# A mixture-of-experts layer on one core: six slots for the high parts of the weights, low parts written over their raw slots, five high parts ahead

## The reference

```
def _moe(h, w_router, b_router, w_gate, w_up, w_down):
    ...
    scores = jax.nn.sigmoid((hf @ w_router).astype(jnp.float32))
    ...
    for e in range(N_EXPERTS):
        he = jax.nn.silu(hf @ w_gate[e]) * (hf @ w_up[e])
        y = y + combine[:, e:e + 1] * (he @ w_down[e])
    return y.reshape(B, T, D).astype(h.dtype)
```

## Time and profile before

| | |
|---|---|
| median of 3 runs | 769.23 us (768.83 to 771.93) |
| span of the profiled execution | 769.4 us |
| PE busy, share of the span | 738.5 us, 96% |
| DVE | 587.7 us, 76% |
| ACT | 429.6 us, 56% |
| POOL | 95.5 us, 12% |
| moved by DMA | 172.72 MB, mean 224 GB/s |

### The profile page before, as it was taken

The page is one execution under the profiler, slowest core; times in us unless marked ns, Lnnn a source line. Parts: engine busy times, 40 slices in busy tenths (PEclk is TensorE's granted clock), DMA queues, the critical chain, the costliest instruction groups (busy, mean ns, idle before and its releaser), DMA issues. The chain is left out here.

```text
span 769.4 us, 10991 instructions
## 1 busy us (share of the span) xinstructions
PE 738.5 (96%) x4051; PEld 601.2 (78%) x4051; DVE 587.7 (76%) x817; ACT 429.6 (56%) x514; POOL 95.5 (12%) x131
## 2 busy tenths in 40 slices
PE   6899999999999999999999989999999999999994
PEld 5777999987877776878888757888888888888872
DVE  6967999797763545434666789888998999899988
ACT  5643344255445454652230246787788778887855
POOL 4010000000110000000000246311121111212002
PEclk9999999999999999999999999999999999999998
DMA  8547313420273111151349949999999999999163
GB/s 282 169 132 257 109 56 110 165 70 1 94 294 110 55 55 56 57 217 55 110 122 388 333 143 363 406 392 402 393 401 391 403 394 393 389 404 385 44 243 137
DMA packets 98547, 172.72 MB, mean 224 GB/s; under 512 B 15264, under 2 KB 35056, under 8 KB 98188
## 3 DMA queue, kind: packets, MB, share of 16 engines
q1 hardware_dynamic: 91200, 153.10, 55.2%
q0 software_dynamic: 4896, 12.95, 4.3%
q10 hardware_dynamic: 2412, 6.15, 2.1%
HBM read 161.83 MB, written 21.10 MB: 238 GB/s over the span
## 5 line engine op out<-in xcount | busy, mean ns | idle before, releaser
L2044 DVE TENSOR_TENSOR m_lo<-m_raw,m_hi 128x2048 fp32r<-128x2048 f32 x95 | 214.9, 2289 | 26.0 <-ACT m_hi L1008 22.9
L1008 ACT ACTIVATE m_hi<-m_raw 128x2048 fp32r<-128x2048 f32 x95 | 179.1, 1917 | 22.9 <-PE low L1156 22.4
L1154 PE MATMUL low<-m_hi,xe_hi 128*128 128x512 f32 x256 | 102.7, 401 | 0.7 <-DVE xe_lo L2180 0.5
L1156 PE MATMUL low<-m_hi,xe_lo 128*128 128x512 f32 x256 | 100.0, 391 | 0.0
L1155 PE MATMUL low<-m_lo,xe_hi 128*128 128x512 f32 x256 | 99.8, 390 | 0.0
L1154 PE MATMUL low<-hT_hi,w_hi 128*128 128x512 f32 (+1 forms) x240 | 94.5, 394 | 3.1 <-ACT smallT L767 1.2
L1155 PE MATMUL low<-hT_lo,w_hi 128*128 128x512 f32 (+1 forms) x240 | 92.0, 383 | 0.0
L1156 PE MATMUL low<-hT_hi,w_lo 128*128 128x512 f32 (+1 forms) x240 | 91.6, 382 | 0.0
L1731 DVE TENSOR_TENSOR w_lo<-raw,w_hi 128x2048 fp32r<-128x2048 f32 x27 | 61.8, 2290 | 37.2 <-ACT w_hi L737 37.0
L737 ACT ACTIVATE w_hi<-raw 128x2048 fp32r<-128x2048 f32 x28 | 53.5, 1909 | 16.5 <-PE wide L1156 8.3
L1154 PEld LDWEIGHTS low<-m_hi,xe_hi 128*128 128x128 f32 x256 | 48.1, 188 | 14.1 <-DVE m_lo L2044 3.7
(11 more groups left out here) (424 smaller groups left out, 1419.7 us busy)
## 6 DMA issues: line engine op xcount, KB each, us to landing
m_raw<-in_w_gate SPq DMA_DIRECT2D x32, 1024.0 KB, 8.0
m_raw<-in_w_up SPq DMA_DIRECT2D x32, 1024.0 KB, 7.9
m_raw<-in_w_down SPq DMA_DIRECT2D x31, 1024.0 KB, 8.3
raw<-in_w_in SPq DMA_DIRECT2D x19, 1024.0 KB, 5.7
raw<-in_w_out SPq DMA_DIRECT2D x4, 1024.0 KB, 5.1
y<-y_dram SPq DMA_DIRECT2D x8, 512.0 KB, 6.5
table_dram<-table_row ACTq DMA_DIRECT2D x1, 2624.0 KB
strips<-table_dram SPq DMA_DIRECT2D x8, 264.0 KB, 4.1
```

Of the source, the lines that this page charges most:

```text
L1008: nc.scalar.activation(m_hi[n % MS][:, :], (m_spare if is_last(n, j) else m_raw[slot])[:, :], ACT.Copy).then_inc(q["m_hi_ready"], 1)
L1154: nc.tensor.matmul(outp, lh, rh, start=first, stop=False)
L1156: return nc.tensor.matmul(outp, ll, rh, start=False, stop=last)
L2044: v.tensor_tensor(m_lo[n % MS][:, :], (m_spare if is_last(n, j) else m_raw[n % MR])[:, :], m_hi[n % MS][:, :].bitcast(F32), ALU.subtract). ...
```

## The change

`MS` goes from 3 to 6. The three new high slots lie where the three low slots were. A low part is now written over its own raw unit, in place; the last one over `m_spare`, under the name `spare_lo`. Since the slot then holds the low part until PE has used it, everything that waited for "low part made" in order to use a raw slot anew waits for "PE has used it": SP's refills, its loads of `g2`, `b2` and of the results, and DVE's `last_sel`. At the start, ACT makes five high parts ahead of the first rows in place of three, and the sixth right behind the first `xe_hi`.

```diff
-MR, MS = 12, 3
+MR, MS = 12, 6
...
-        m_hi = [at(f"m_hi{i}", [P, UNIT], F32R, x) for i, x in enumerate((A0 + 8, A0 + 16, A0 + 24))]
-        m_lo = [at(f"m_lo{i}", [P, UNIT], F32R, x) for i, x in enumerate((0, 8, 16))]
+        m_hi = [at(f"m_hi{i}", [P, UNIT], F32R, x) for i, x in enumerate((A0 + 8, A0 + 16, A0 + 24, 0, 8, 16))]
+        m_lo = [at(f"m_lo{i}", [P, UNIT], F32R, A0 + (32 + 8 * i if i < MR - 1 else 0)) for i in range(MR)]
+        spare_lo = at("spare_lo", [P, UNIT], F32R, A0 + 136.5)
...
                 for slot in range(MR):
                     e, part = order[MR + slot]
-                    sp.wait_ge(q["m_lo_ready"], j * MR + (slot + 1 - MR))
+                    sp.wait_ge(q["m_used"], j * MR + (slot + 1 - MR))
                     m_load(j * 2 + (e - 2), part, slot)
             for slot in range(MR - 1):
                 u = MU * NE - MR + slot
-                sp.wait_ge(q["m_lo_ready"], u + 1 - MR)
+                sp.wait_ge(q["m_used"], u + 1 - MR)
                 m_load(*order[u], slot)
 
-            sp.wait_ge(q["m_lo_ready"], MU * NE - MR + 7)
+            sp.wait_ge(q["m_used"], MU * NE - MR + 7)
...
             sp.wait_ge(q["all_scattered"], 1)
-            sp.wait_ge(q["m_lo_ready"], MU * NE - MR + 4)
+            sp.wait_ge(q["m_used"], MU * NE - MR + 4)
             results_load()
...
-            m_split_hi(0)
-            m_split_hi(1)
-            m_split_hi(MS - 1)
+            for n in range(MS - 1):
+                m_split_hi(n)
...
-            m_split_hi(3)
+            m_split_hi(MS - 1)
             silu_gate(0, 2)
-            m_split_hi(4)
             act.wait_ge(q["xe_done"], 2)
...
-            def m_unit(u, s, outp, part, x_hi, x_lo):
+            def m_unit(u, n, outp, part, x_hi, x_lo, low=None):
 
                 pe.wait_ge(q["m_lo_ready"], u)
-                wh = m_hi[s][:, :].rearrange("p (c n) -> p c n", c=4)
-                wl = m_lo[s][:, :].rearrange("p (c n) -> p c n", c=4)
+                wh = m_hi[n % MS][:, :].rearrange("p (c n) -> p c n", c=4)
+                wl = (low or m_lo[n % MR])[:, :].rearrange("p (c n) -> p c n", c=4)
...
                 dve.wait_ge(q["m_hi_ready"], j * MR + (n + 1))
-                v.tensor_tensor(m_lo[n % MS][:, :], (m_spare if is_last(n, j) else m_raw[n % MR])[:, :], m_hi[n % MS][:, :].bitcast(F32), ALU.subtract).then_inc(q["m_lo_ready"], 1)
+                v.tensor_tensor((spare_lo if is_last(n, j) else m_lo[n % MR])[:, :], (m_spare if is_last(n, j) else m_raw[n % MR])[:, :],
+                                m_hi[n % MS][:, :].bitcast(F32), ALU.subtract).then_inc(q["m_lo_ready"], 1)
...
             for i in range(3):
                 m_split_lo(MU + i, j)
-            dve.wait_ge(q["m_lo_ready"], MU * NE - 4)
+            dve.wait_ge(q["m_used"], MU * NE - 4)
             v.tensor_tensor(last_sel[:, :, :], count_up[:, :].rearrange("p (o x) -> p o x", o=1).to_broadcast([P, TT, P]),
```

More of the change, by code:

```diff
@@ L536, in _ @@
             with sp.If(over > P):
-                sp.wait_ge(q["m_lo_ready"], 6 * NE)
+                sp.wait_ge(q["m_used"], 6 * NE)
                 sp.wait_ge(q["part_ready"], 4)
@@ L1077, in _ @@
             nc.scalar.activation(xe_hi[:, 0:4, :], bank[6][:, :].rearrange("p (c x) -> p c x", c=4), ACT.Copy).then_inc(q["xe_half_hi"], 1)
-            m_split_hi(5)
             act.wait_ge(q["m_used"], 4)
@@ L1621, in _ @@
                 pe.wait_ge(q["xe_lo_ready" if u else "xe_half_lo"], 1)
-                m_unit(u + 1, u % MS, bank[u // 2][:, :], u % 2, xe_hi, xe_lo)
+                m_unit(u + 1, u, bank[u // 2][:, :], u % 2, xe_hi, xe_lo)
             hidden(0)
@@ L1628, in expert_pe @@
                 pe.wait_ge(q["xe_lo_ready"], j * 2 + (2 + s))
[L1629 to L1632, removed]
+                m_unit(j * MR + (n - 1), n - 2, bank[0][:, :], 0, xe_hi, xe_lo)
+                m_unit(j * MR + n, n - 1, bank[0][:, :], 1, xe_hi, xe_lo)
+                m_unit(j * MR + (n + 1), n, bank[1][:, :], 0, xe_hi, xe_lo)
+                m_unit(j * MR + (n + 2), n + 1, bank[1][:, :], 1, xe_hi, xe_lo)
                 tokens(s, j * 16 + 32)
@@ L1636, in expert_pe @@
                 pe.wait_ge(q["y_out"], j * 2 + (1 + s))
-                m_unit(j * MR + (n + 3), 2, bank[4][:, :], None, hd_hi, hd_lo)
-                m_unit(j * MR + (n + 4), 0, bank[5][:, :], None, hd_hi, hd_lo)
+                m_unit(j * MR + (n + 3), n + 2, bank[4][:, :], None, hd_hi, hd_lo)
+                m_unit(j * MR + (n + 4), n + 3, bank[5][:, :], None, hd_hi, hd_lo)
                 hidden(e)
@@ L1646, in _ @@
             pe.wait_ge(q["xe_lo_ready"], NE)
-            m_unit(u, 1, bank[0][:, :], 0, xe_hi, xe_lo)
-            m_unit(u + 1, 2, bank[0][:, :], 1, xe_hi, xe_lo)
+            m_unit(u, u - 1, bank[0][:, :], 0, xe_hi, xe_lo)
+            m_unit(u + 1, u, bank[0][:, :], 1, xe_hi, xe_lo)
             pe.wait_ge(q["hd_lo_ready"], NE - 1)
             pe.wait_ge(q["y_out"], NE - 1)
[L1651 to L1654, removed]
+            m_unit(u + 2, u + 1, bank[4][:, :], None, hd_hi, hd_lo)
+            m_unit(u + 3, u + 2, bank[5][:, :], None, hd_hi, hd_lo)
+            m_unit(u + 4, u + 3, bank[1][:, :], 0, xe_hi, xe_lo)
+            m_unit(u + 5, u + 4, bank[1][:, :], 1, xe_hi, xe_lo)
             pe.wait_ge(q["hid_ready"], NE)
@@ L1667, in _ @@
             pe.wait_ge(q["m_lo_ready"], u + 6)
-            wh, wl = (t[1][:, :].rearrange("p (c n) -> p c n", c=4) for t in (m_hi, m_lo))
+            wh, wl = (t[(u + 5) % len(t)][:, :].rearrange("p (c n) -> p c n", c=4) for t in (m_hi, m_lo))
             for k in range(4):
@@ L1672, in _ @@
             mm.then_inc(q["m_used"], 1)
-            m_unit(u + 7, 2, bank[5][:, :], None, hd_hi, hd_lo)
+            m_unit(u + 7, u + 6, bank[5][:, :], None, hd_hi, hd_lo, spare_lo)
             pe.wait_ge(q["lists_ready"], 6)
```

## The result

| | kernel before | changed kernel |
|---|---|---|
| median of the runs | 770.02 us (768.83 to 773.43, 22 runs) | 772.06 us (769.64 to 773.54, 22 runs) |
| ratio | | 1.0018, 95% interval [1.0010, 1.0026] |
| span of the profiled execution | 769.4 us | 770.2 us |

The change makes the kernel slower by a little: the ratio is 1.4 us, the means of these runs are 1.3 us apart and their medians 2.0. Three sets of runs together (46 of the changed kernel) have a mean of 771.64 us; 138 runs of the kernel before have 770.34 and a median of 770.15. The distance of the means is 1.3 us (95% interval 1.0 to 1.6). The forecast was 769.8 us, range 768.2 to 771.4: the median lies 0.7 above the range.

A forecast was written before the change was run, and what follows sets the result against it. PE was taken to bound the expert loop and DVE the end. Terms 0 + 0 + 0 + 0.6 = +0.6 us on 769.4 gave 770.0 us for a profile, 769.8 us for the runs, range 768.2 to 771.4.

The forecast's parts named there:

- The base of the sum: Whole kernel: profiled span 769.4 us, median of three runs 769.23, so the runs' forecast was put at 769.8 us.
- the term for the end: End of the program: `last_sel`'s later wait delays PE's unit 93 and so the last store, +0.6 us, bounds 0 to 1.4.
- Forecast +0.65 at `hid`: Last expert: low part 93 late, PE starts unit 93 0.56 us later, its first matmul holds 0.09 more.
- no longer held by the result loads: End: the last `part` begins at 745.1 us, following PE instead of waiting for the result loads.
- Six slots: Expert loop: ACT's 22.4 us of waits on PE go, PE notices nothing; 0 us, bounded by PE's 3.7 us.
- Rival 1: Expert loop: the 0.09 us gap per expert closes, gaining 1.2 to 3.7 us; 766.1 to 768.6 us, chance 0.07.
- the rule of the Trainium skill: Expert loop: a repeating gap on the saturated engine can mean too few buffers; twice the slots would gain 1.2 to 3.7 us.
- which no buffer frees: Expert loop: the late high part stands behind `ye` and `hd_hi` in ACT's order, so more slots gain 0 us.
- Five high parts ahead: Start: two more pieces of 1.9 us fit in ACT's idle 7.84 us, leaving 4 us of cover; 0 us.
- low part in place: DVE: the low part written over its raw slot keeps its instruction shape, 2.29 us each; 0 us.
- later refills: SP's weight loads: issued 2.8 to some 5 us later, with a lead of 30.6 us, 17 us over; 0 us.
- rival 2: Weight loads: refills on PE's count land after their high part is due; 789 us, or +5 for one, chance 0.05.

The follow-up runs named there:

- experiment 2: Changed kernel with `last_sel` moved behind low part 93: 770.74 us, ratio 1.0005 (before 770.30); its repeat 769.75 us, ratio 1.0000 (before 770.27).
- 1: Kernel before with one edit, `last_sel` waits until PE has used unit 91: 770.79 us, ratio 1.0002; again 770.69 us, ratio 1.0011.
- 4: Kernel before plus one unused DVE subtract of two SBUF operands behind low part 93: 770.70 us, ratio 1.0003 (before 770.30).
- 3: Changed kernel with `last_sel` behind low part 93, three high slots and ACT's old order at the start: 770.19 us, ratio 0.9997.
- the old start of 9 to 12: Changed kernel with `last_sel` behind low part 93 and three high parts ahead at the start, six slots kept: 770.35 us, ratio 1.0000.

## Why the prediction failed

**The base of the sum was wrong.** This is the step that failed: "the median of the runs is 769.23, so nothing to speak of lies around it", from which the 769.8 was made. 769.23 was a median of three runs. Over 138 runs the kernel's median is 770.15, 0.9 above it. And something does lie around the span: in each of the 269 runs whose span is known (as 770.0 with a span of 768.3), the time is the span plus 1.7 to 1.9 us. So a span of 769.4 meant a run of 771.2 us, one of the longer ones; it was read as the middle. That the span exceeded the median of the runs, which it is a part of, should have told me that this profile and that median didn't belong together. With 770.15 the same working gives 770.8 us for the changed kernel, and a range of the same width, 769.2 to 772.4, would have held the result.

The base is not the whole miss of 2.3 us (772.06 - 769.8), though. It is 0.9 of it, and the term for the end another 0.15. Of the other 1.2, 0.4 is that this comparison's median lies above the 771.65 of all 46 runs, and some 0.7 is distance between the two kernels for which the sum had nothing and the traces show nothing: forecast +0.6, traces +0.75, medians of all runs +1.5, means +1.3. That part stays open.

**`last_sel`: right mechanism, a term slightly too small.** Forecast +0.65 at `hid`; the trace has 0.56: PE's unit 93 began 0.43 late (3.15 - 2.72) and not 0.56, and its first matmul held PE 0.33 us, 0.10 more, as reckoned. Forecast 1.4 later relative to PE: 734.73 against PE's 734.53, so 0.20 behind unit 92, where it was 1.22 ahead (733.04 against 734.26): 1.42. PE's new wait for low part 93 came. What the sum left out is POOL: "no longer held by the result loads" was wrong, since they came 0.8 us later themselves. The end costs 0.75 us over eleven profiles (0.65 in the first pair), 0.15 more than the sum's 0.6.

**Six slots: right, 0.** The waits of ACT went from 22.4 us to none, and PE's stayed at 13. Rival 1, and the rule of the Trainium skill (Perfetto Trace Analysis, Optimization Strategy) on gaps that repeat, did not happen by more buffers alone: PE's busy time in the ten-expert window went from 178.42 to 178.50 us, and the timed runs of experiment 2 and its repeat lie 0.1 us from before. But the rule was half right. It was the order on ACT that held the late part, as the prediction had it; that order could be changed only with more slots. With three, high part n+6 needs PE to be done with unit n+3, for which `ye` itself waits, so it can't stand ahead of `ye`. I stopped at "which no buffer frees" and didn't ask what the buffers would allow.

**Five high parts ahead, low part in place, later refills: right, 0.** The first `xe_hi` came at 457.26 (457.29 before); ACT's idle time ahead of it fell from 7.84 to 4.26 us, so 3.6 of the cover was used. The 0 of these parts holds in the traces; whether the open distance of the timed runs belongs to one of them isn't shown. ACT at the start:

```profile
442.38 9.10 ACT L1009 ACTIVATE m_hi<-m_raw 128x2048 fp32r<-128x2048 f32 x5
451.50 1.28 ACT L1045 ACT_TABLE_LOAD   x1
457.26 0.60 ACT L1070 ACTIVATE xe_hi<-wide 128x512 fp32r<-128x512 f32 x1 [4.26 <-PE wide L1579]
```

SP's weight loads wait for PE now, as forecast, and no high part waits for them: ACT has no wait for a load of `m_raw` in the stage (rival 2 did not happen). SP's queue in the stage:

```profile
SPq L496 <- PE low L1154: 155.1, 57, 24.8
SPq L496 <- PE wide L1154: 69.1, 26, 3.3
```

**What stays open.** The traces give the changed kernel +0.75 us, the runs +1.3 (1.0 to 1.6). The slow pace of the loop (243.88 in place of 243.54, 0.35 us) showed in all five profiles of the changed kernel and of it with `last_sel` moved, in three of five of the kernel before and its two variants (1 and 4), and in neither of the two with the old start (3 and the old start of 9 to 12). If that is no accident, early high parts bring it about more often, and it adds up to 0.1 to 0.2 us on average; twelve profiles don't prove it, and `last_sel` moved with the new start is not slower for it in the runs (+0.1). Nor does the clock's dip at 50 us, ahead of all that the edits touch, look like the reason. The timed runs have no trace, but each has its mean granted clock: 0.9923 over the 46 runs of the changed kernel, 0.9921 over the 116 of the kernel before for which it is known. About 0.4 us of the distance of the means has no place (1.3 - 0.75 - 0.15; with the interval, 0.1 to 0.7).

## What to carry to other kernels

A wait that moves from one's own counter to that of another engine costs what stands behind it in the in-order queue, not the instruction itself: put such an instruction behind the one that somebody waits for (one line, 0.75 us). More buffers take away waits, but not order; when a gap survives them, look which instruction stands ahead of the late one, and whether the new buffers now let it pass (1.6 us here, where the slots alone gave nothing). And before a sum is made in tenths, see that the base is known to tenths: hold the profile's span against the runs, and distrust a median of three.

## What the runs showed of the hardware

- **A DVE instruction with two SBUF operands holds up POOL's scatter.** The DMA_INDIRECT takes 0.97 us when DVE idles, 1.87 when it starts 1.3 us into a low part, 1.70 beside a subtraction of 128x1024, 1.16 beside `last_sel`, and ends 0.85 us behind the DVE instruction each time. A DVE instruction with one operand in PSUM doesn't: in the kernel before, a gather takes 1.00 us in the middle of an `xe_lo`. A 128x1 copy on POOL shows both: 1.87 us when a low part had just begun (it ends with it), 0.20 beside an `hd_lo`, which reads PSUM:

```profile
504.75 1.00 POOL L640 DMA_INDIRECT xg<-h_dram,now_source  x1 [0.79 <-POOL now_source L637]
504.44 1.22 DVE L2120 TENSOR_TENSOR xe_lo<-wide,xe_hi 128x1024 fp32r<-128x1024 f32 x1
...
708.91 1.87 POOL L696 COPY now_result<-result_row 128x1 int32<-128x1 int32 x1
708.45 6.81 DVE L2044 TENSOR_TENSOR m_lo<-m_raw,m_hi 128x2048 fp32r<-128x2048 f32 x3 [0.85 <-ACT m_hi L1008]
...
725.80 0.20 POOL L696 COPY now_result<-result_row 128x1 int32<-128x1 int32 x1
725.58 0.69 DVE L2129 TENSOR_TENSOR hd_lo<-low,hd_hi 128x512 fp32r<-128x512 f32 x1
```

  The Trainium skill (SBUF — State Buffer, Terms) says that DVE and GpSimd share a pair of ports that is locked for a whole instruction, and that the loser blocks. By that rule the traces agree.
- **The same code has two or three paces.** PE's granted clock at 50 to 55 us is 0.67 to 0.75 in some executions and 1.00 in others (1.2 to 1.6 us for the same kernel), at 446 to 458 us 0.86 or 1.00 (0.8 us). In the first profile of before each dip is some 3 us at the lower level (rows of 0.50, 1.2 GHz), behind 2 to 3 us in which PE was busy for a quarter to two thirds of the time (47 to 49 and 448 to 451 us); its second profile has such a pause at 47 to 49 us too, and no dip behind it. The loop takes 243.54 or 243.88 us with a granted clock of 0.99 or 1.00 in either. What sets the last wasn't found.
